# Rotary rows gathered by small on-chip transfers, and six smaller reorderings, in a two-block transformer kernel

## What is computed (the reference, cut)

```
def partial_rope(x, cos, sin):
    half = ROPE_DIM // 2
    x1 = x[..., :half]
    x2 = x[..., half:ROPE_DIM]
    return jnp.concatenate([x1 * cos - x2 * sin, x2 * cos + x1 * sin, x[..., ROPE_DIM:]], axis=-1)
...
    qa = partial_rope(heads(qa, N_HEADS_A), cos_h, sin_h)
    ka = partial_rope(heads(ka, N_HEADS_A), cos_h, sin_h)
    qi = partial_rope(qi.reshape(B, L, IDX_HEADS, IDX_DIM), cos_h, sin_h)
    ki = partial_rope(ki, cos, sin)
```

## Time and profile before

| what | value |
|---|---|
| median of 3 runs | 1526.36 us (1525.99 to 1527.17) |
| the profiled execution, its own time | 1525.9 us |
| span of that execution, first to last instruction | 1524.0 us |
| mean granted clock of TensorE | 0.996 |
| PE busy | 1481.7 us, 97% |
| VectorE busy | 859.7 us, 56% |
| ScalarE busy | 618.5 us, 41% |
| GpSimd busy | 617.3 us, 41% |

### The profile page before, as it was taken

One profiled execution on the slowest core, in us unless ns is written; L12 is line 12 of the kernel. 1 busy time (PEld: TensorE's weight loads), 2 busy tenths in 40 slices (PEclk: granted clock), 3 DMA queues, 4 the chain that ended last, 5 costly groups with the idle time before them and its releaser, 6 DMA issues.

```text
span 1524.0 us, 22037 instructions
## 1 busy us (share of the span) xinstructions
PE 1481.7 (97%) x9049; PEld 1191.6 (78%) x9049; DVE 859.7 (56%) x1479; ACT 618.5 (41%) x1031; POOL 617.3 (41%) x452
## 2 busy tenths in 40 slices
PE   7999999999999999999999999989998999999997
PEld 6887776887888788887777777767888888888886
DVE  4895676136874467437348995477567422233324
ACT  6322665354223276554334235545544321222222
POOL 6454211444464211543523531223464435544441
PEclk9999999999999999999999999999999999999999
DMA  9485200234533110242313231111242323323331
GB/s 365 132 299 181 56 29 29 89 128 171 201 112 104 57 58 31 98 138 83 107 51 100 69 110 50 57 34 56 85 151 70 111 94 100 96 98 98 96 96 70
DMA packets 86214, 158.45 MB, mean 104 GB/s; under 512 B 2737, under 2 KB 20833, under 8 KB 86113
## 3 DMA queue, kind: packets, MB, share of 16 engines
q1 hardware_dynamic: 82256, 148.91, 29.5%
q10 hardware_dynamic: 3856, 8.12, 1.5%
HBM read 154.90 MB, written 2.12 MB: 103 GB/s over the span
## 4 chain that ended last, share of the span: by engine, by line
PE 75%; DVE 18%; ACT 2%; DMA 2%; POOL 1%; issue 1%; DVEq 0%; SPq 0%; ACTq 0%
PE banks L506 10%; PE banks L508 10%; PE banks L507 10%; PE banks L502 7%; PE banks L504 7%; PE banks L503 7%; PE banks L621 4%; PE banks L623 3%; PE banks L622 3%; PE banks L674 2%; PE banks L662 2%; DVE slots L2084 2%; DVE max L2082 2%; PE banks L646 2%; DVE work_lo L1838 2%; DVE ev L1838 2%
## 5 line engine op out<-in xcount | busy, mean ns | idle before, releaser
L480 POOL TENSOR_TENSOR w_lo<-w_raw,w_hi 128x512 fp32r<-128x512 f32 x436 | 595.8, 1400 | 858.3 <-ACT w_hi L1086 781.0
L1086 ACT ACTIVATE w_hi<-w_raw 128x2048 fp32r<-128x2048 f32 (+1 forms) x111 | 208.9, 1882 | 202.4 <-DMA w_raw<-w_ff_dram 141.3
L502 PE MATMUL banks<-xh,w_hi 128*128 128x512 f32 x640 | 250.3, 391 | 0.0
L504 PE MATMUL banks<-xh,w_lo 128*128 128x512 f32 x640 | 249.0, 389 | 0.0
L503 PE MATMUL banks<-xl,w_hi 128*128 128x512 f32 x640 | 249.0, 389 | 0.0
L506 PE MATMUL banks<-w_hi,xh 128*128 128x512 f32 x384 | 152.7, 398 | 11.4 <-POOL w_lo L468 9.3
L506 PE MATMUL banks<-w_hi,yh 128*128 128x512 f32 x384 | 150.2, 391 | 0.3 <-DVE yl L1969 0.2
L507 PE MATMUL banks<-w_lo,xh 128*128 128x512 f32 x384 | 150.4, 392 | 0.0
L508 PE MATMUL banks<-w_hi,xl 128*128 128x512 f32 x384 | 150.4, 392 | 0.0
L508 PE MATMUL banks<-w_hi,yl 128*128 128x512 f32 x384 | 149.5, 389 | 0.0
L507 PE MATMUL banks<-w_lo,yh 128*128 128x512 f32 x384 | 149.4, 389 | 0.0
(11 more groups left out here) (311 smaller groups left out, 2453.0 us busy)
## 6 DMA issues: line engine op xcount, KB each, us to landing
w_raw<-w_ff_dram SPq DMA_DIRECT2D x32, 1024.0 KB, 5.2
w_raw<-w_in_dram SPq DMA_DIRECT2D x22, 1024.0 KB, 5.1
work_hi<-w_ada_dram SPq DMA_DIRECT2D x16, 1024.0 KB, 7.7
w_raw<-rec_w_in_dram SPq DMA_DIRECT2D x16, 1024.0 KB, 5.4
w_raw<-att_w_in_dram SPq DMA_DIRECT2D x14, 1024.0 KB, 6.1
work_lo<-w_ada_dram SPq DMA_DIRECT2D x8, 1024.0 KB, 8.1
w_raw<-ple_w_gate_dram SPq DMA_DIRECT2D x8, 1024.0 KB, 5.1
w_raw<-att_w_out_dram SPq DMA_DIRECT2D x4, 1024.0 KB, 5.0
```

The costliest lines, as they stand in the source:

```text
L480: ins = pool.tensor_tensor(wlo[s][:, k, :], raw[s][:, k, :], wh[s][:, k, :].bitcast(F32), ALU.subtract)
L502: pe.matmul(out, w_h, x_h, start=start, stop=False)
L504: return pe.matmul(out, w_l, x_h, start=False, stop=stop)
L1086: act.activation(wh[s][:, 0:kn, :], raw[s][:, 0:kn, :], ACT.Copy).then_inc(w_split, 1)
```

## The change

It has seven parts.
1. *Start.* The first two pairs of x and weight columns are loaded as pieces of 256 KB. PE takes, for the first of the eight steps, the four high-times-high products, then those with x's low halves, then those with w's, each behind its own wait. The Silu, the identity's load and the table's preload are moved; `h` is loaded two chunks later; the third cast of weights stands ahead of the squares.
2. *SP's order* of the second layer's weights and the last modulation chunks.
3. *POOL* waits for six of the eight gated additions before it splits the first chunk of tv1 and of tv2.
4. *qka2.* The permutation products and their evacuations are gone. The 16 rotated features of each of the two heads of a tile are copied by transfers into `ev` rows, once as they are (16 rows) and once with the halves swapped (two times 8 rows): six transfers for a tile, 24 for a group, all on ACT's queue, 2 KB a row. DVE turns a group's 128 rows with three operations, `rope_of_group`, and eight transfers bring them back. Two constant tables for the gathered rows are loaded. PE and DVE wait for all 16 transfers back before the top attention.
5. *The last search* is finished ahead of the top attention, and the first stick-breaking product is made ahead of the top attention's last output.
6. *In gb2* ACT copies the gate's tile out (`gates_moved`) ahead of the cast of the next weights (`high_after`).
7. *Semaphores* of two row loads are joined; `ki_ready` is now `roped`.

The diff, cut:

```diff
-    ("tv2", TV, 2, 0, 0), ..., ("qka2", "A" * 16, 4, 8, 0),
+    ("tv2", TV, 2, 0, 0), ..., ("qka2", "A" * 8, 4, 0, 0),
+ROPE_OUT, ROPE_BACK = 24, 8
+        rope_rows = [slot["D"][:, 3584:4096], slot["A"][:, 0:T]]
...
-            for j in range(4):
+            for k in range(2):
+                sp.dma_start(x_cols[:, k, :], a["c_x_cols"][k * P:k * P + P, :]).then_inc(sg(f"first_in{k}"), 16)
+                s = slot_of() if k == 0 else 0
+                sp.dma_start(raw[0][:, k, :], win0[k * P:k * P + P, first[0]:first[0] + G]).then_inc(sg(f"first_in{k}"), 16)
+            for j in range(1, 4):
...
-            sp.dma_start(h[:, :, :], a["x"][0].rearrange("(t p) d -> p t d", p=P)).then_inc(sg("x_in"), 16)
             n_ada = 0
             for adas in (0, 0, 3, 0, 0, 2, 3, 3, 1, 3):
...
                 load(cols(win0, first[count[0] // 2], k0=4 * (count[0] % 2)))
+                if count[0] == 3:
+                    sp.dma_start(h[:, :, :], a["x"][0].rearrange("(t p) d -> p t d", p=P)).then_inc(sg("x_in"), 16)
...
                 pool.wait_ge(w_split, c - 1)
+                if c in (BASE["tv1"][1], BASE["tv2"][1]):
+                    pool.wait_ge(sg("pg0_h" if c == BASE["tv1"][1] else "pg1_h"), 6)
...
-            for k in range(KT):
+            pe.wait_ge(sg("first_hi"), 2)
+            for m in range(TT):
+                pe.matmul(bank(n0 + m), xh[:, 0, m * P:m * P + P], wh[0][:, 0, :], start=True, stop=False)
+            pe.wait_ge(sg("x_lo"), 1)
...
+            pe.wait_ge(sg("v_lo"), 1)
...
+            for k in range(1, KT):
                 pe.wait_ge(sg("x_lo"), k + 1)
                 pe.wait_ge(sg("v_lo"), k + 1)
...
-            for g in range(2):
-                rope_group(n0 + 8 * g, c0 + 2 * g)
...
+            groups("qka2", 2, True)
+            groups("b2", 2, True)
             all_banks_free("merge2")
+            pe.wait_ge(sg("rope_back"), 32 * ROPE_BACK)
...
+            def rope_out(g, m):
+
+                x, (r, w) = feat["B"][:, 4 * g + m, :], [ev[:, 2 * g + j, :] for j in range(2)]
+                for hh in range(2):
+                    at_, to_ = HD * hh, 32 * m + 16 * hh
+                    act.dma_start(r[to_:to_ + 16, :], x[at_:at_ + 16, :]).then_inc(sg(f"rope_out{g}"), 16)
+                    for b in (0, 8):
+                        act.dma_start(w[to_ + b:to_ + b + 8, :], x[at_ + 8 - b:at_ + 16 - b, :]).then_inc(sg(f"rope_out{g}"), 16)
+
+            def rope_back(g):
+
+                act.wait_ge(sg("roped"), g + 2)
+                for m in range(4):
+                    for hh in range(2):
+                        at_, to_ = 32 * m + 16 * hh, HD * hh
+                        act.dma_start(feat["B"][to_:to_ + 16, 4 * g + m, :], ev[at_:at_ + 16, 2 * g, :]).then_inc(sg("rope_back"), 16)
+
+            def rope_group(g, scale):
+                n = BASE["qka2"][0] + 4 * g
+                high_after("qka2", 2 * g)
                 for m in range(4):
-                    empty(n + 4 + m, dst(m))
+                    empty(n + m, feat["B"][:, 4 * g + m, :], scale=scale)
+                    if m > 0:
+                        act.wait_ge(*emptied(n + m - 1))
+                        rope_out(g, m - 1)
+                act.wait_ge(*emptied(n + 3))
+                rope_out(g, 3)
+                high_after("qka2", 2 * g + 1)
...
+            act.dma_start(rope_rows[0], a["c_cos_rows"]).then_inc(sg("rope_in"), 16)
+            act.dma_start(rope_rows[1], a["c_sin_rows"]).then_inc(sg("rope_in"), 16)
+            act.wait_ge(ev_free, BASE["qka2"][2] + 4)
+            rope_group(0, HD ** -0.5)
+            rope_group(1, 1.0)
+            rope_back(0)
             empty_groups("b2", 1, lambda m: feat["D"][:, m, :], scale=HD ** -0.5)
-            act.wait_ge(ev_free, BASE["qka2"][2] + 12)
+            rope_back(1)
             empty_groups("b2", 1, lambda m: feat["D"][:, 4 + m, :], skip=4)
...
                     gates_moved(tiles_done(t - 2) if t > 1 else 0, tiles_done(t - 1))
+                if t > 0 and t % 3 == 0:
+                    high_after("gb2", t // 3 - 1)
...
-                if t % 3 == 2:
-                    high_after("gb2", t // 3)
...
+            def rope_of_group(g):
+
+                r, w = ev[:, 2 * g, :], ev[:, 2 * g + 1, :]
+                dve.wait_ge(sg(f"rope_out{g}"), 16 * ROPE_OUT)
+                V.mark(dve.tensor_tensor(r, r, rope_rows[0], ALU.mult))
+                V.after(dve.tensor_tensor(w, w, rope_rows[1], ALU.mult))
+                dve.tensor_tensor(r, r, w, ALU.add).then_inc(sg("roped"), 1)
+
             choose(2)
-            for m in range(4):
-                rope_tile(n + 12 + m, u + 4 + m, feat["B"][:, 4 + m, :])
-            choose(3, 0, 15)
+            rope_of_group(0)
+            choose(3, 0, 12)
+            rope_of_group(1)
+            choose(3, 12)
             dve.wait_ge(*emptied(BASE["merge2"][0] - 1))
+            dve.wait_ge(sg("rope_back"), 32 * ROPE_BACK)
...
             def last_strip(part):
 
-                if part == 0:
-                    choose(3, 15, 16)
-                    compare(3)
...
                 if part == 3:
                     dve.wait_ge(sg("strict_in"), 16)
                     stick_mask(0)
                     stick_mask(1)
+                    stick_products(0)
...
-            stick_products(0)
             for t in range(STK_STEPS):
```

More of the change, by code:

```diff
@@ L69 @@
     *out_stages(1, [("modt", "A", 0, 0, 0)]),
-    ("tv2", TV, 2, 0, 0), ("qi2", "AAAAAAADDDAA", 2, 4, 0), ("vb2", "AAAAAAA" * 4, 2, 0, 0), ("qka2", "A" * 16, 4, 8, 0),
+    ("tv2", TV, 2, 0, 0), ("qi2", "AAAAAAADDDAA", 2, 4, 0), ("vb2", "AAAAAAA" * 4, 2, 0, 0), ("qka2", "A" * 8, 4, 0, 0),
     ("b2", "A" * 8, 4, 0, 0), ("ga2", "", 4, 0, 0), ("gb2", "", 4, 0, 0), ("merge2", "A" * 16, 4, 16, 8),
@@ L425, in _ @@
             load_ada(19)
+            load(cols(win1, D))
             load_ada(20)
-            load(cols(win1, D))
+            load(cols(win1, D, k0=4))
             load_ada(21)
             load_ada(22)
-            load(cols(win1, D, k0=4))
+            load(cols(win1, D + G))
             load_ada(23)
-            for c0 in (D + G, 0, G):
-                load_groups(win1, 1, c0)
+            load(cols(win1, D + G, k0=4))
+            load_groups(win1, 2)
             load_beside(win1, 3 * D)
@@ L699, in _ @@
             n0 = BASE["tv0"][0]
-            for k in range(KT):
+            pe.wait_ge(sg("first_hi"), 2)
+            for m in range(TT):
+                pe.matmul(bank(n0 + m), xh[:, 0, m * P:m * P + P], wh[0][:, 0, :], start=True, stop=False)
+            pe.wait_ge(sg("x_lo"), 1)
+            for m in range(TT):
+                pe.matmul(bank(n0 + m), xl[:, 0, m * P:m * P + P], wh[0][:, 0, :], start=False, stop=False)
+            pe.wait_ge(sg("v_lo"), 1)
+            for m in range(TT):
+                pe.matmul(bank(n0 + m), xh[:, 0, m * P:m * P + P], wlo[0][:, 0, :], start=False, stop=False)
+            for k in range(1, KT):
                 pe.wait_ge(sg("x_lo"), k + 1)
@@ L1294, in _ @@
             act.dma_start(small[:, :], a["c_small"]).then_inc(sg("small_in"), 16)
[L1295 removed]
+            act.preload_act_table_set("silu_and_others")
             act.wait_ge(sg("small_in"), 16)
[L1297 to L1298 removed]
             for k in range(KT):
[L1300 removed]
+                act.wait_ge(sg(f"first_in{k if k < 2 else k // 2 + 1}"), 32 if k % 4 < 2 else 16)
                 act.activation(xh[:, k, :], x_cols[:, k, :], ACT.Copy, scale=gain0[:, k:k + 1]).then_inc(sg("first_hi"), 1)
@@ L1305, in _ @@
             highs[0] = 2
+            act.dma_start(ident[:, :], a["c_ident"]).then_inc(const_in, 16)
+            A.after(act.activation(stat[:, 40:48], c_col, ACT.Silu))
+            act.sem_inc(sg("c_silu"), 1)
             act.dma_start(wfl, a["c_w_fl"].rearrange("p (k n) -> p k n", k=KT)).then_inc(sg("fl_in"), 16)
@@ L1309, in _ @@
             act.preload_act_table_set("sqrt_and_others")
+            high(2)
             act.wait_ge(sg("x_in"), 16)
@@ L1313, in _ @@
                 root("tv0", stat[:, 32 + m:33 + m], stat[:, 8 + m:9 + m], eps)
-            high(2)
             high(3)
@@ L2144, in stick_mask @@
                    .then_inc(sg("stk_masked"), 1)
-            attention("top", 4, lambda q: isc[:, KOFF[q]:KOFF[q] + (q + 1) * P], top_s, output_of_top, last_strip)
             def stick_products(t):
@@ L2161, in stick_products @@
                 dve.tensor_tensor(att, att, rest[:, :, 1:w], ALU.mult).then_inc(sg("stk_att"), 1)
+            attention("top", 4, lambda q: isc[:, KOFF[q]:KOFF[q] + (q + 1) * P], top_s, output_of_top, last_strip)
             def stick_split(i):
@@ L2285, in constants @@
         perm[:HD, 1, base:base + HD] = np.eye(HD, dtype=np.float32)
+    rows = [HD * head + f for _ in range(4) for head in range(2) for f in range(16)]
     return {
@@ L2288, in constants @@
         "c_strict": strict, "c_cos": fcos, "c_sin": fsin, "c_perm": perm.reshape(P, 3 * P),
```

(1 more changed line is left out.)

69 lines of the change are left out of this document (18 added, 51 removed).

## The result

The changed kernel takes 1530.16 us (median of 18 executions, 1526.81 to 1533.65); the kernel before, beside it, 1526.80. The ratio is 1.0023, with an interval of 1.0016 to 1.0030: slower, by a quarter of a per cent, where 10.6 us less were forecast. The profiled execution is the fastest of the 18, 1526.81 with a span of 1525.0 and a mean granted clock of 0.993; the other executions show 0.989 to 0.992, so that what its rows show of the clock is the least that was lost.

What follows compares the result with a forecast made beforehand. PE, busy 1481.7 of 1524.0 us, was taken to bound the kernel. Terms -2.5 + 1.5 + 1.0 - 2.7 - 0.7 - 5.3 - 1.9 = -10.6 gave 1515.7 us by the median, range 1507 to 1522.

Steps and rivals of the forecast that it cites:

- Start: First x and weight columns: smaller pieces let PE begin near 6.4 instead of 9.35; taken as -2.5 us.
- POOL held back: At tv1 and tv2: additions end earlier, but POOL's window slows tiny root instructions; +1.5 and +1.0 us.
- Removed products: In qka2: eight permutation products and their evacuations go, 3.4 us per group, 6.8 for both.
- Top attention's start: PE's wait for the first probabilities (L662) falls from 1.95 to about 1.25 us: -0.7.
- Stick-breaking: First stick-breaking turn: the 3.63 us wait goes, and 1.7 us of half clock behind it: -5.3.
- Gate tiles: Gate tiles copied ahead of the cast: three PE waits of 0.64 us go, -1.9.
- rival (e): Top attention: DVE's chain takes over through late gathered rows, so the gain is gone: 1526 or so; chance 0.05.
- the issues in qka2: 24 issues per group on ACT's queue at 0.48 us delay cast and POOL; PE stands 2.05 us twice, +4.1.
- the prediction's own formula: In qka2: with p us from issue to issue, the stall per group is 24p - 9.5, 2.05 at 0.48.
- Rival (c): Clock falls at new idle stretches, tv1 and two in qka2, 1.7 us apiece: up to 1520.8; chance 0.20.
- rival (d): ACT's queue clogs in qka2: from p = 0.70 stalls eat all other gains; 1531 at 0.8; chance 0.05.
- a little longer issues: Part of the range's high end, 1522: rival (c) with tv1's worse end or slightly longer issues.

Runs made afterwards that it cites:

- both casts ahead: Changed kernel without POOL's wait, with casts moved ahead of the transfers out in qka2 and ahead of the first transfers back: 1508.46 us, ratio 0.9878.
- the cast ahead: Changed kernel with each qka2 group's cast for the next second half moved behind the third evacuation, ahead of tiles 1 to 3's transfers out: 1515.47 us, 0.9924.
- the kernel with four per tile: Changed kernel with four transfers out per tile in place of six, partner rows in one unswapped transfer of 16 rows: 1515.90 us, ratio 0.9923.

## Why the prediction was wrong

Most of its steps stood. *PE's busy time bounds the kernel*: what the rows explain of the times is work taken from PE, a wait of PE, or its clock behind one. *Start*, -2.5: 2.6, with some luck: the first product came 3.2 to 3.4 us earlier and not 2.95, and part of it seems to be lost again at the modulation's sums at 137, which the forecast did not have. *POOL held back*, +1.5 and +1.0: the waits rose by 1.42 and 1.17, through 1.2 us per tiny instruction, as forecast; in the time three pairs of kernels differ by 0.7 to 3.6 us, none of them clear of the noise. *Removed products*, -6.8: with both casts ahead the groups follow each other by the 21.76 us that the forecast took. *Top attention's start*, -0.7: 1.95 became 1.03, and the wait for the first scores rose by 0.1. *Stick-breaking*, -5.3: 5.3; the wait is exact, but the clock behind it took 2.7 us in that profile and not 1.7, so the last digit is luck. *Gate tiles*, -1.9: three waits of 0.64. *DVE's chain* has time in hand, rival (e) fell.

One term failed, that of the issues in qka2: "An issue occupies that queue 0.45 us, and two follow each other by 0.48". The place was right, and so was the path (issue, cast, POOL, PE, twice), and the prediction's own formula gives the measured waits from the measured pitch: 24 x 0.69 - 9.5 = 7.1 (7.35), 24 x 0.64 - 9.5 = 5.9 (6.10). But 0.48 was the pitch of two loads from DRAM (a third, just ahead of them at 751.33, took 0.34); the change copies on the chip, at 0.64 to 0.69. The stalls are 13.4 us instead of 4.1. The eight transfers back, which the prediction let cost nothing because the cast behind them is wanted half a group later, cost nothing while PE was late; with the first cast ahead they made PE wait 3.0 us at 881.

That term had a second half, which stood among the rivals alone: the clock. Rival (c) priced its fall for stalls of 2 us, rival (d) priced long stalls without it. The stalls of 6 to 7 us brought it down each time (7.35 and 6.10 here, 7.37 and 6.54 in the kernel without POOL's wait), here for 4.5 us of work. So (d) decides not from p = 0.70 but where 2 x (24p - 9.5) + 4.5 eats 14.7, at p = 0.61. With both corrected the sum is -10.6 + 9.3 + 4.5 = +3.2: 1529.6 by the median, and 1530.16 was measured. That they agree so well is partly luck: both corrections are read from the profiled execution, which took 1526.81 where the sum gives it 1529.1, and the others, with lower mean clocks, took more. Rival (d) had a chance of 0.05, with rows 7's own outlier of 2.88 in its favour; no row of the trace showed a copy from the chip to the chip, so the price was unknown on the dear side, and the range's end of "a little longer issues" gave it almost nothing.

The rule that was weighed in the prediction, the Trainium skill's "DMA: Bandwidth & Descriptors", Rules for kernel authors (few large transfers instead of many small ones), points the right way: fewer issues with the same bytes gave 14.3 us. What was paid here is not the fixed part of each transfer's landing, though. It is the time for which the issuing engine's own queue is held: with the cast ahead the same 48 transfers went out and both waits were gone, and in the changed kernel DVE goes from its search to the gathered rows without a wait (16 and 6 us behind the last issues). The section Anatomy of one DMA, from which the prediction took 2.0 us and 50 ns, stands on that page of the Trainium skill under GpSimd's path; the transfers here are issued from ACT, and their issues took 0.54 to 0.65 us.

## What to carry to other kernels

A transfer is an instruction in the program order of the engine that issues it: count the issues, multiply by a pitch measured for that kind of transfer, and look for what stands behind them on that engine. If that is what feeds the bound engine, move it ahead of the issues; here one moved cast took away 14.7 us, and a second one a wait of 3.0 more. In these profiles waits of PE of about 2 to 3 us were followed by either level of the clock, and all from 3.27 us on, but the one at the start, by the lower: a forecast should price a stall of 2 to 3 us at both levels, and one as long as those at the lower.

## What the runs showed of the hardware that was not expected

- Issuing a copy from on-chip memory to on-chip memory held ACT's queue 0.54 us for 16 rows of 2 KB and 0.65 for 8 rows in the changed kernel (medians; some of 8 rows took up to 1.18), and 0.61 for most of the 16-row issues in the kernel with four per tile; the same shapes read from DRAM took mostly 0.32 to 0.34.
- Of 41 waits of PE of 1.88 to 3.03 us in these profiles, 22 were followed by the lower clock and 19 were not. The turn's 2.15 at tv1 kept 1.00 in the changed kernel and fell to 0.50 in the one with the cast ahead, whose instructions up to there are the same; 1.95 at the top attention's start kept the clock in the kernel before, and 1.94 at the same place in the changed kernel with the old rotation was followed by 0.50; 3.03 at 881 kept it in the kernel with the cast ahead, and 2.96 there did not in the one with the cast ahead and without POOL's wait. The thirteen waits of 3.27 to 7.37 us in these profiles, other than those for the first product, were all followed by 0.50.
- With several such waits in a kernel its executions differ by a few us: the 18 of the changed kernel lie between 1526.8 and 1533.7, with mean clocks of 0.993 in the fastest and 0.989 in the slowest.
